# Filler products on TensorE around eight RMS norms of a three-block trunk

## The chip, the core and the metric

The kernel runs on one core of a Trainium2 chip. The time is that of one execution on the device, in microseconds (us); lower is better. TensorE is called PE here, VectorE DVE, ScalarE ACT, GpSimd POOL and SyncE SP. PEclk, the granted clock, is the share of full speed that the throttle granted to PE: 1.00 is 2.4 GHz and 0.50 is 1.2 GHz.

## What is computed

Two transformer layers over 256 context and 256 latent tokens of width 1024, then a third block of another kind. Each stage begins with an RMS norm and a modulation:

```python
def rmsnorm(x, w):
    x32 = x.astype(jnp.float32)
    r = lax.rsqrt(jnp.mean(x32 * x32, axis=-1, keepdims=True) + EPS)
    return (x32 * r).astype(x.dtype) * w

def trunk_layer(xl, xc, ...):
    xl = xl + 0.5 * g1l * swiglu(modulate(rmsnorm(xl, norm_w[0]), sh1l, sc1l), w_ffn1_in, w_ffn1_out)
    ...
    mix_l, mix_c = token_mixer(modulate(rmsnorm(xl, norm_w[1]), ...), ...)   # attention and a short convolution
    xl = xl + g2l * mix_l
    xl = xl + 0.5 * g3l * swiglu(modulate(rmsnorm(xl, norm_w[2]), sh3l, sc3l), w_ffn2_in, w_ffn2_out)
```

After the two layers comes a final norm. The third block takes its result: norm, two scans (mLSTM and HGRN) behind one input projection, output projection, norm, a feed-forward part with a convolution, final norm. In all there are ten norms.

## The kernel before

Everything is feature-major: x is 8 chunks (kc, 0 to 7) of 128 features by 512 tokens, in SBUF all the time. The weights come from HBM as units of 1 MB into a ring of three buffers (raw). SP starts the DMA for a unit when PE has begun the one that used its buffer (semaphore unit_begun). ACT splits each half of a unit into a high part (w_hi, line 877) and DVE into a low part (w_lo, line 1256), and PE makes three products for each chunk, high by high, high by low and low by high (split_product, lines 412 and 420). A product of 512 columns starts every 0.23 us, one of 256 every 0.12 us.

Each engine runs its own instruction list in the order written, and semaphores join them. PE's list is written by hand in the order of the stages.

A norm goes so. While the product before it still runs, DVE adds each finished chunk into x (line 1362, semaphore x_updated), ACT squares it (line 894, square_ready), and POOL adds the squares of chunks 0 to 5 into square_sum (line 1829, square_added). At the end of the product PE calls norm_sum. It sums over features by products with a column of ones, one for each 128 tokens (line 463, one column each, into bank 4): first POOL's sum (k = 0), then the squares of chunk 6 (k = 1), then those of chunk 7 (k = 2). ACT takes the root (line 904), DVE the reciprocal (1288) and four diagonal blocks of it (1290), and PE multiplies ones by these blocks, which spreads the factor over all partitions (line 471, "the spread", bank 5). DVE then scales x chunk by chunk (1309), ACT and DVE modulate (915, 1314), ACT makes the high part of h (919) and DVE the low part (1320). PE meanwhile runs joint_product (line 441): two weight halves side by side, each new chunk of h used as soon as it is there, the second half two chunks behind the first, 48 products in all.

The ten norms in order are norm10, norm20, norm30, norm11, norm21, norm31, final1, norm_a, norm_b and final2. norm31, final1, norm_b and final2 work on the 256 latent tokens alone (two blocks of 128 instead of four). The joint stage of norm21 has 256 columns, and that of norm_a 512 for one half and 256 for the other. norm_a follows final1 with no product between them. Behind norm_b comes no joint_product but f32 products straight from h and raw (line 821).

An f32 product stands in the trace as two records, each with its own weight load. Lines 463, 471 and 821 therefore have twice as many records as the code has products.

The eight PSUM banks are assigned by hand. Banks 2, 3, 6, 7, 0, 1, 2, 3 hold the eight chunks of a product ahead of a norm (OUT_BANK), so bank 6 holds the third. UPDATED[name] is how many updates of x stand ahead of a norm, and each adds 8 to x_updated.

Of the kernel before, what the change touches and what calls it, by code (L numbers as in the profile page):

```python
# [31 lines left out]
P = 128  # L32
D = 1024
KC = D // P
# [89 lines left out]
def build_program(nc, stream, x_in, ctx2_in, params_in, consts_in, out, until=None):  # L124
    with ExitStack() as stack:
        def sb(name, shape):
            return stack.enter_context(nc.sbuf_tensor(name, shape, F32))
# [8 lines left out]
        consts = sb("consts", [P, N_CONSTS])  # L136
# [17 lines left out]
        bank = [stack.enter_context(nc.psum_tensor(f"bank{b}", [P, 512], F32)) for b in range(8)]  # L154
        sems = {}

        def sem(name):
            if name not in sems:
                sems[name] = stack.enter_context(nc.semaphore(name))
            return sems[name]  # L160
# [5 lines left out]
        def const(name, a=0, n=None, rows=P):  # L166
            first, width = CONSTS[name]
            return consts[0:rows, first + a:first + a + (width - a if n is None else n)]

        ident, ones = const("ident"), const("ones")  # L170
# [8 lines left out]
        x_updated = sem("x_updated")  # L179
# [6 lines left out]
                 for i in range(DEPTH) for n in range(3)]  # L186
        NORMS += [("final1", 3 * DEPTH, CTX), ("norm_a", 3 * DEPTH + 1, 0), ("norm_b", 3 * DEPTH + 2, CTX),
                  ("final2", 3 * DEPTH + 3, CTX)]
        NORM_AT = {name: n for n, (name, _, _) in enumerate(NORMS)}
        UPDATED = {name: updates for name, updates, _ in NORMS}  # L190
        START = {name: t0 for name, _, t0 in NORMS}
        OUT_BANK = (2, 3, 6, 7, 0, 1, 2, 3)
        PAIR_BANKS = ((0, 1), (2, 3), (6, 7))
        ROW_BANK, TURN_BANK = 4, 5
        HEAD_NORM_BANK = (0, 1, 4, 5)
        SUM_BANK, SPREAD_BANK = 4, 5
        norm_rms, norm_rinv = small[:, 64:68], small[:, 68:72]
        ADDED = KC - 2
        square_sum = rinv
# [2 lines left out]
        def earlier(name, counts):  # L202

            return sum(1 for n, (other, _, t0) in enumerate(NORMS) if n < NORM_AT[name] and counts(other, t0))
# [8 lines left out]
        def joint(name):  # L213

            return name[:5] in ("norm1", "norm2", "norm3") or name == "norm_a"

        def diags_before(name):

            return sum((T - t0) // P for _, _, t0 in NORMS[:NORM_AT[name]])
# [158 lines left out]
        def _(pe):  # L378
# [71 lines left out]
            def normed(t0):  # L450
                return (lambda kc: h_hi[:, kc, t0:]), (lambda kc: h_lo[:, kc, t0:])

            def norm_sum(name):


                n, t0 = NORM_AT[name], START[name]
                for k, part in enumerate((square_sum, squares[:, 2, :], squares[:, 3, :])):
                    if k == 0:
                        pe.wait_ge(sem("square_added"), (ADDED - 1) * (n + 1))
                    else:  # L460
                        pe.wait_ge(sem("square_ready"), KC * n + ADDED + k)
                    for tc in range((T - t0) // P):
                        last = nc.tensor.matmul(bank[SUM_BANK][:, tc:tc + 1], part[:, t0 + tc * P:t0 + (tc + 1) * P], ones[:, 0:1],  # L463
                                                start=k == tc == 0, stop=k == 2, skip_group_check=True)
                        if k == tc == 0 and joint(name):
                            last.then_inc(half_begun, 1)
                last.then_inc(sem("norm_summed"), 1)
                if name == "norm10":
                    pe.wait_ge(sem("side_done"), FIRST_SIDES)
                pe.wait_ge(sem("diag_ready"), diags_before(name) + (T - t0) // P)  # L470
                nc.tensor.matmul(bank[SPREAD_BANK][:, 0:T - t0], ones, norm_diag[:, 0:T - t0], start=True, stop=True)\  # L471
                    .then_inc(sem("rinv_spread"), 1)

            def swiglu(name, norm, norm_after):
                f, t0 = FFNS.index(name), START[norm]
# [36 lines left out]
            def down(name, update, hidden_before, sides, t0, norm_after):  # L512

                before = KC * BANKED.index(update)
                operand = (lambda kc: hidden_hi[:, kc, t0:]), (lambda kc: hidden_lo[:, kc, t0:])
                for j in range(4 * len(GROUPS)):
                    at = AT[f"down{name}", j]
                    g, pair_of_chunks = j % len(GROUPS), j // len(GROUPS)
                    if j < sides:
                        side_sum(at - 1)  # L520
                    full_wait(pe, at)
                    pe.wait_ge(sem("hidden_ready"), hidden_before + min(KC * (g + 1), FC) if j < len(GROUPS) else hidden_before + FC)
                    if j == 3 * len(GROUPS):
                        pe.wait_ge(x_updated, before_updates(update) + 2)
                    for sub in range(2):
                        c = 2 * pair_of_chunks + sub
                        last = split_product(bank[OUT_BANK[c]][:, 0:T - t0], At.half, operand, GROUPS[g], KC * g, sub == 0,
                                             g == 0, g == len(GROUPS) - 1)
                        if g == len(GROUPS) - 1:
                            last.then_inc(sem("acc_ready"), 1)  # L530
                        if sub == 0 and j < sides:
                            side_turn(At.side)
                            At.side += 1
                norm_sum(norm_after)

            def out_product(name, update, t0, norm_after, await_chunk=None):

                for j in range(4):
                    full_wait(pe, AT[name, j])
                    if j == 0 and await_chunk:  # L540
                        for last in joint_product([bank[OUT_BANK[sub]][:, 0:T - t0] for sub in range(2)], [normed(t0)] * 2, await_chunk):
                            last.then_inc(sem("acc_ready"), 1)
                        continue
                    if j == 3:
                        pe.wait_ge(x_updated, before_updates(update) + 2)
                    for sub in range(2):
                        split_product(bank[OUT_BANK[2 * j + sub]][:, 0:T - t0], At.half, normed(t0), KC, 0, sub == 0)\
                            .then_inc(sem("acc_ready"), 1)
                norm_sum(norm_after)
# [294 lines left out]
            side_turn(FIRST_SIDES - 1)  # L844
            At.side = FIRST_SIDES
            norm_sum("norm10")
            for i in range(DEPTH):
                swiglu(f"1{i}", f"norm1{i}", f"norm2{i}")
# [1179 lines left out]
```

## Time and profile before

| | us |
|---|---|
| median of 3 runs | 2535.13 |
| lowest and highest | 2529.25, 2537.61 |
| span of the profiled execution | 2530.4 |
| PE busy in it | 2386.8 (94%) |
| DVE, ACT, POOL busy | 1163.3, 930.1, 172.2 |
| mean granted clock of PE | 0.969 |

The profiled execution is known by its span, from its first to its last instruction. That is 4.7 us under the median of the runs. A matmul record includes the time through the pipeline, so records of one engine overlap; the distance between their starts tells what a product costs.

### The profile page before, as it was taken

What the parts mean: (1) busy time and instruction counts of PE and PEld (TensorE: products, weight loads), DVE (VectorE), ACT (ScalarE), POOL (GpSimd) and SP (SyncE); (2) the same over time, 40 slices, a digit from 0 to 9 for tenths busy, and PEclk for the clock granted to TensorE, in tenths of its full rate; (3) what the DMA queues carried; (4) which work ended last, traced back from release to release, by engine and by line L of the source; (5) the groups of instructions that cost most, each with busy time, mean ns of one, the idle gap of its engine ahead of it and who ended that gap; (6) DMA issues with size and microseconds to landing.
All of it is one profiled execution on the core that took longest, in us unless ns stands there. A gap on an engine that the chain in (4) does not pass through costs nothing.

```text
span 2530.4 us, 34867 instructions
## 1 busy us (share of the span) xinstructions
PE 2386.8 (94%) x13140; PEld 1927.3 (76%) x13140; DVE 1163.3 (46%) x2058; ACT 930.1 (37%) x1446; POOL 172.2 (7%) x115
## 2 busy tenths in 40 slices
PE   6999999999999999999999999999997997789998
PEld 3777777784777777777777787779996876558888
DVE  2233222436643333224333224675545666656884
ACT  3333322323443333224333223356644364332333
POOL 1000000005010000010000000310001003101001
PEclk9999999999999999999999998999998998889999
DMA  6444445220134444443444433314553221004444
GB/s 241 166 166 166 166 167 191 88 88 34 35 116 166 166 166 166 169 185 129 166 166 166 166 117 112 121 67 150 182 196 104 100 100 67 1 26 141 150 148 167
DMA packets 47643, 340.50 MB, mean 135 GB/s; under 512 B 5184, under 2 KB 6208, under 8 KB 6592
## 3 DMA queue, kind: packets, MB, share of 16 engines
q1 hardware_dynamic: 47280, 338.19, 36.2%
q8 instruction: 64, 1.05, 0.2%
q0 software_dynamic: 272, 1.05, 0.1%
q14 instruction: 27, 0.22, 0.0%
HBM read 338.16 MB, written 1.05 MB: 134 GB/s over the span
## 4 chain that ended last, share of the span: by engine, by line
PE 89%; DVE 6%; ACT 2%; issue 1%; POOL 1%; DMA 0%; SPq 0%; DVEq 0%; ACTq 0%; POOLq 0%
PE bank L412 44%; PE bank L420 21%; PE bank L821 6%; PE bank L389 4%; PE bank L441 3%; PE bank L401 1%; PE bank L663 1%; PE bank L463 1%; PE bank L642 1%; DVE h L1601 1%; PE bank L622 1%; PE bank L651 1%; PE bank L619 1%; ACT w_hi L877 1%; PE bank L471 1%
## 5 line engine op out<-in xcount | busy, mean ns | idle before, releaser
L1256 DVE TENSOR_TENSOR w_lo<-raw,w_hi 128x1024 fp32r<-128x1024 f32 (+1 forms) x389 | 469.1, 1206 | 895.0 <-ACT w_hi L877 894.4
L877 ACT ACTIVATE w_hi<-raw 128x1024 fp32r<-128x1024 f32 (+1 forms) x389 | 403.3, 1037 | 853.9 <-DMA raw<-stream 436.8
L412 PE MATMUL bank<-h_hi,w_hi 128*128 128x512 f32 (+1 forms) x2024 | 709.7, 363 | 3.1 <-ACT w_hi L877 1.7
L412 PE MATMUL bank<-h_lo,w_hi 128*128 128x512 f32 (+1 forms) x2024 | 695.1, 356 | 0.0
L412 PEld LDWEIGHTS bank<-h_hi,w_hi 128*128 128x128 f32 x2024 | 383.6, 190 | 81.6 <-issue 28.3
L420 PE MATMUL bank<-h_hi,w_lo 128*128 128x512 f32 (+1 forms) x2024 | 429.8, 355 | 5.2 <-DVE w_lo L1256 5.2
L412 PEld LDWEIGHTS bank<-h_lo,w_hi 128*128 128x128 f32 x2024 | 383.9, 190 | 50.5 <-issue 0.5
L420 PEld LDWEIGHTS bank<-h_hi,w_lo 128*128 128x128 f32 x2024 | 341.3, 189 | 58.9 <-DVE w_lo L1256 6.0
L412 PE MATMUL bank<-hidden_hi,w_hi 128*128 128x512 f32 (+1 forms) x880 | 298.6, 354 | 2.5 <-ACT w_hi L877 2.5
L412 PE MATMUL bank<-hidden_lo,w_hi 128*128 128x512 f32 (+1 forms) x880 | 293.7, 348 | 0.0
L412 PEld LDWEIGHTS bank<-hidden_hi,w_hi 128*128 128x128 f32 x880 | 167.4, 190 | 32.8 <-issue 13.2
L420 PE MATMUL bank<-hidden_hi,w_lo 128*128 128x512 f32 (+1 forms) x880 | 182.0, 347 | 2.0 <-DVE w_lo L1256 2.0
L412 PEld LDWEIGHTS bank<-hidden_lo,w_hi 128*128 128x128 f32 x880 | 167.6, 190 | 19.5
L420 PEld LDWEIGHTS bank<-hidden_hi,w_lo 128*128 128x128 f32 x880 | 145.4, 190 | 22.8 <-DVE w_lo L1256 2.2
L821 PE MATMUL bank<-h,raw 128*128 128x256 f32 x704 | 153.9, 382 | 1.3 <-DVE h L1314 1.3
L821 PEld LDWEIGHTS bank<-h,raw 128*128 128x128 f32 x704 | 134.9, 192 | 20.6 <-issue 2.0
L1741 DVE SCALAR_TENSOR_TENSOR arena<-arena,params 128x189 f32<-128x189 f32 (+2 forms) x352 | 122.9, 427 | 20.2 <-ACT arena L1177 20.2
L1829 POOL TENSOR_TENSOR rinv<-squares 128x512 f32<-128x512 f32 (+1 forms) x10 | 15.1, 1514 | 1663.3 <-ACT squares L894 1663.3
L389 PE MATMUL bank<-raw,cond 128*32 128x256 f32 x1536 | 109.7, 406 | 18.2 <-DMA raw<-stream 14.5
L885 ACT ACTIVATE side_row<-bank 128x256 f32<-128x256 f32 x96 | 36.9, 385 | 242.3 <-PE bank L389 224.5
L1264 DVE TENSOR_TENSOR mod_ada<-bank,params 128x4 f32 (+1 forms) x72 | 11.7, 163 | 186.6 <-PE bank L401 186.6
L389 PEld LDWEIGHTS bank<-raw,cond 128*32 128x32 f32 x1536 | 41.6, 113 | 69.3 <-issue 34.6
(220 smaller groups left out, 2227.5 us busy)
## 6 DMA issues: line engine op xcount, KB each, us to landing
raw<-stream SPq DMA_DIRECT2D x318, 1024.0 KB, 4.8
x<-x_in SPq DMA_DIRECT2D x1, 2048.0 KB, 10.2
consts<-consts_in SPq DMA_DIRECT2D x1, 1121.5 KB, 5.8
x<-ctx_in POOLq DMA_DIRECT2D x1, 1024.0 KB, 6.1
out<-x SPq DMA_DIRECT2D x2, 512.0 KB, 3.0
params<-params_in SPq DMA_DIRECT2D x1, 413.5 KB, 3.2
```

The lines of the kernel that those rows point to most:

```text
L389: last = nc.tensor.matmul(bank[ROW_BANK][g:g + 32, 0:UNIT], cond[:, which, kc, :], raw[at % RING][:, kc, :], start=kc < 4, stop=kc >= 4)
L401: last = nc.tensor.matmul(bank[TURN_BANK][:, 2 * q:2 * q + 2], side_row[:, q * P:(q + 1) * P], const("sum_rows"), start=True, stop=True)
L412: last = nc.tensor.matmul(acc, w_hi[:, buffer, kc, :], v(first_chunk + kc), start=start and kc == n == 0, stop=False)
L420: last = nc.tensor.matmul(acc, w_lo[:, buffer, kc, :], hi(first_chunk + kc), start=False, stop=stop and kc == chunks - 1)
L441: last[sub] = nc.tensor.matmul(accs[sub], w[:, (At.half + sub) % 2, kc, :], v(kc), start=kc == n == 0, stop=kc == KC - 1 and n == 2)
L463: last = nc.tensor.matmul(bank[SUM_BANK][:, tc:tc + 1], part[:, t0 + tc * P:t0 + (tc + 1) * P], ones[:, 0:1], start=k == tc == 0, stop=k = ...
L471: nc.tensor.matmul(bank[SPREAD_BANK][:, 0:T - t0], ones, norm_diag[:, 0:T - t0], start=True, stop=True)\
L821: last = nc.tensor.matmul(bank[PAIR_BANKS[j][gv]][:, 0:LAT], raw[at % RING][:, kc, gv * P:(gv + 1) * P], h[:, kc, CTX:], start=kc == 0, st ...
L877: nc.scalar.activation(w_hi[:, buffer, 0:chunks, :], raw[at % RING][:, 0:chunks, sub * P:(sub + 1) * P], ACT.Copy)\
L885: nc.scalar.activation(side_row[:, :], bank[ROW_BANK][:, 0:UNIT], ACT.Copy).then_inc(sem("side_row"), 1)
L1256: nc.vector.tensor_tensor(w_lo[:, buffer, 0:chunks, :], raw[at % RING][:, 0:chunks, sub * P:(sub + 1) * P], w_hi[:, buffer, 0:chunks, :].b ...
L1741: nc.vector.scalar_tensor_tensor(acc[:, ro, co], source[:, ri, ci], w, acc[:, ro, co], ALU.mult, ALU.add)\
```

## The change

norm_sum gets filler products at three places, for the eight norms ahead of which x was updated, except final2: norm20, norm30, norm11, norm21, norm31, final1, norm_a and norm_b. A filler multiplies the identity by 256 columns of constants, in f32, into bank 6, which nobody reads before it is written anew. Two stand between the sum with k = 0 and the wait for the sum with k = 1, four between the sums and the wait for the spread's diagonals, and eight behind the spread. A new wait at the top of norm_sum holds PE until four of the eight chunks have been added into x, so that bank 6 is free.

```diff
+        KEEP_BANK = 6
+        KEEP = (2, 4, 8)
...
+            def keep_running(count):
+
+                for _ in range(count):
+                    nc.tensor.matmul(bank[KEEP_BANK][:, 0:2 * P], ident, consts[:, 0:2 * P], start=True, stop=True)
+
             def norm_sum(name):
 
 
                 n, t0 = NORM_AT[name], START[name]
+                busy = UPDATED[name] > 0 and name != "final2"
+                if busy:
+                    pe.wait_ge(x_updated, KC * UPDATED[name] - 4)
                 for k, part in enumerate((square_sum, squares[:, 2, :], squares[:, 3, :])):
                     if k == 0:
                         pe.wait_ge(sem("square_added"), (ADDED - 1) * (n + 1))
                     else:
+                        if k == 1 and busy:
+                            keep_running(KEEP[0])
                         pe.wait_ge(sem("square_ready"), KC * n + ADDED + k)
...
                 last.then_inc(sem("norm_summed"), 1)
+                if busy:
+                    keep_running(KEEP[1])
                 if name == "norm10":
                     pe.wait_ge(sem("side_done"), FIRST_SIDES)
                 pe.wait_ge(sem("diag_ready"), diags_before(name) + (T - t0) // P)
                 nc.tensor.matmul(bank[SPREAD_BANK][:, 0:T - t0], ones, norm_diag[:, 0:T - t0], start=True, stop=True)\
                     .then_inc(sem("rinv_spread"), 1)
+                if busy:
+                    keep_running(KEEP[2])
```

## Rows read from the trace of the kernel before

**Rows 1.** The page: the span, busy times by engine, the chain by engine.
```profile
span 2530.4 us, 34867 instructions
...
PE 2386.8 (94%) x13140; PEld 1927.3 (76%) x13140; DVE 1163.3 (46%) x2058; ACT 930.1 (37%) x1446; POOL 172.2 (7%) x115
...
PE 89%; DVE 6%; ACT 2%; issue 1%; POOL 1%; DMA 0%; SPq 0%; DVEq 0%; ACTq 0%; POOLq 0%
```

**Rows 2.** Waits of PE, whole span: total us, times, longest us.
```profile
PE bank L471 <- DVE rms L1290: 13.8, 10, 1.6
...
PE bank L463 <- POOL rinv L1829: 9.8, 1, 9.8
```

**Rows 3.** Timeline, norm11: start us, us, engine, line, operation [idle before <-releaser].
```profile
1143.05 0.95 PE L463 MATMUL bank<-consts,rinv 128*128 128x1 f32 x8
1143.86 2.04 PE L463 MATMUL bank<-consts,squares 128*128 128x1 f32 x16
1147.44 2.08 PE L471 MATMUL bank<-rms,consts 128*128 128x512 f32 x2 [1.54 <-DVE rms L1290]
...
1152.14 0.76 PE L441 MATMUL bank<-h_hi,w_hi 128*128 128x512 f32 x1 [2.62 <-ACT h_hi L919]
...
1159.65 0.69 DVE L1320 TENSOR_TENSOR h_lo<-squares,h_hi 128x512 fp32r<-128x512 f32 x1
...
1165.28 0.39 PE L441 MATMUL bank<-h_lo,w_hi 128*128 128x512 f32 x1
```

**Rows 4.** Stretches: us, busy of PE, PEld, DVE, ACT, POOL, then PEclk, DMA, GB/s.
```profile
471.00:471.50 0.50, 0.27 (x2) 0.18 (x1) 0.00 (x0) 0.19 (x2) 0.00 (x0) 0.50 0.00 0
...
717.50:719.50 2.00, 0.62 (x6) 0.53 (x5) 1.01 (x6) 1.21 (x2) 0.00 (x0) 1.00 0.00 0
...
724.30:729.50 5.20, 5.20 (x12) 3.50 (x13) 5.20 (x11) 4.05 (x8) 0.00 (x0) 0.50 0.57 202
...
1716.90:1726.40 9.50, 7.78 (x29) 6.54 (x30) 9.23 (x25) 3.40 (x9) 0.00 (x0) 0.50 0.35 113
...
1927.30:1932.50 5.20, 5.20 (x24) 5.18 (x24) 0.00 (x0) 0.00 (x0) 0.00 (x0) 0.50 0.00 0
...
2294.20:2300.00 5.80, 4.54 (x10) 3.22 (x11) 4.57 (x14) 0.00 (x0) 0.00 (x0) 0.50 0.12 24
```

**Rows 5.** Groups by line and shape, PE: busy us, mean ns | idle before.
```profile
L821 PE MATMUL bank<-h,raw 128*128 128x256 f32 x704 | 153.9, 382 | 1.3 <-DVE h L1314 1.3
```

**Rows 6.** Timeline, norm31: sums, spread, last joint product.
```profile
1714.53 1.19 PE L463 MATMUL bank<-consts,squares 128*128 128x1 f32 x8
1716.86 1.22 PE L471 MATMUL bank<-rms,consts 128*128 128x256 f32 x2 [1.14 <-DVE rms L1290]
...
1728.98 0.28 PE L441 MATMUL bank<-h_lo,w_hi 128*128 128x256 f32 x1
```

**Rows 7.** Timeline, final1 and norm_a.
```profile
1915.11 0.61 PE L463 MATMUL bank<-consts,squares 128*128 128x1 f32 x4 [0.24 <-ACT squares L894]
1916.79 0.70 PE L471 MATMUL bank<-rms,consts 128*128 128x256 f32 x2 [1.07 <-DVE rms L1290]
1927.29 1.86 PE L463 MATMUL bank<-consts,rinv 128*128 128x1 f32 x8 [9.81 <-POOL rinv L1829]
...
1934.14 2.07 PE L471 MATMUL bank<-rms,consts 128*128 128x512 f32 x2 [1.58 <-DVE rms L1290]
```

**Rows 8.** Timeline, norm_b: spread, first products of line 821, last chunks of h.
```profile
2294.17 1.22 PE L471 MATMUL bank<-rms,consts 128*128 128x256 f32 x2 [1.14 <-DVE rms L1290]
2296.66 3.69 PE L821 MATMUL bank<-h,raw 128*128 128x256 f32 x8 [1.26 <-DVE h L1314]
...
2300.03 0.74 DVE L1314 TENSOR_SCALAR h<-h,scales,mod_mod 128x256 f32<-128x256 f32 x2
```

**Rows 9.** Timeline, norm30: spread and last joint product.
```profile
719.66 2.00 PE L471 MATMUL bank<-rms,consts 128*128 128x512 f32 x2 [1.54 <-DVE rms L1290]
...
737.90 0.39 PE L441 MATMUL bank<-h_lo,w_hi 128*128 128x512 f32 x1
```

## Prediction

> **What bounds the kernel now.** I read the page first: PE is busy for 94% of the span and carries 89% of the chain that ended last [rows 1], so what PE does is the time, and at a norm the question is only what PE waits for. The waits of PE come next. Before the spread product (line 471) it waited for DVE's diagonals, 13.8 us over ten norms, and once 9.8 us for POOL's sum of squares [rows 2]. Then I went through each norm by its timeline. Norm11 stands for four alike (norm20, norm30, norm11, norm21: 512 columns). Its sums (line 463) run from 1143.05 to 1145.9, the spread comes 1.54 us later and takes 2.08 us, the first product of the joint stage comes 2.62 us after that, and the last of its 48 products starts at 1165.28 [rows 3]. Last I cut the time by granted clock. It was 1.00 up to the end of the sums, or nearly, and 0.50 (1.2 GHz instead of 2.4) in the spread, in the wait behind it and in the first microseconds of the joint products [rows 4]. At norm_a the sums ran back to back for 5.2 us and the clock stayed at 0.50, so those one-column products did not bring it back, while the dense products of lines 441 and 821 did [rows 4].
>
> **What is added and its price.** Eight norms get 2, 4 and 8 fillers (norm20, norm30, norm11, norm21, norm31, final1, norm_a, norm_b): 112 products; norm10 and final2 get none. A filler is an f32 product of 128 by 128 with 256 columns. The same form stands in line 821: 704 records, two for each product, in 153.9 us [rows 5], so 153.9 / 352 = 0.44 us each. At half clock eight records took 3.69 us [rows 8], 0.85 us for a product after the first. So the three places cost PE 0.87, 1.75 and 3.50 us at full clock, and up to 1.7, 3.4 and 6.8 us at half clock. The new wait on x_updated asks for half of the chunks, while the wait right behind it needs the squares of six of them: it ends earlier, I count it as nothing, and if it did cost its place is ahead of the sums in each norm. Bank 6 has been read by then, so nobody waits for the fillers but PE's own queue.
>
> **First place, 2 fillers between the first sum and the second.** In the full-width norms there is no wait to fill: the 24 records of line 463 follow each other without idle time, as in norm11 [rows 3]. All 0.87 us goes on the path, with bounds of 0.55 (norm20, where the clock fell inside the old sums already and part of that comes back) and 0.87. Four norms: 3.2 us. In the half-width ones the third sum waited 0.24 us for ACT [rows 7], so 0.87 minus about 0.3 = 0.57. At norm_a PE comes from 9.81 us of idling at half clock and the squares are long there [rows 7]: 1.7 us.
>
> **Second place, 4 fillers between sums and spread.** Here there is a real wait, 1.54 us by the records plus about 0.17 of pipeline end [rows 3]: at full clock 1.75 fills it with 0.05 over. In the half-width norms the wait is 1.07 to 1.14 plus 0.17 [rows 6, 7], so 0.45 us too much. At half clock the four take 3.4 us and delay the spread by 1.7.
>
> **What it should give back.** Spread at full clock: a half-width one took 0.70 us at final1 at clock 1.00 and 1.22 us at norm31 [rows 6, 7]; 0.52 us less, and twice that, 1.04, for 512 columns. Joint stage of the four: in norm11 the sixth chunk's low part is ready at 1160.34 [rows 3], 22 products stand behind it at 0.228 us each, 5.0 us, which gives 1165.4; the stage ended at 1165.51. So norm11 has 0.1 us to gain, and I take the same for norm20. In norm30, at half clock for over 5 us of it [rows 4], the last product starts 16.24 us after the spread's end, in norm11 15.76 us [rows 3, 9]: 0.5 us. Norm21, half-width in its joint stage, I put beside norm30: 0.5. That is 1.2 us in all. Here the expected gift is mostly absent: DVE's pace of 1.52 us a chunk hides the slow products.
>
> **Third place, 8 fillers after the spread.** PE was idle there for 2.62 us [rows 3]; 3.50 us make the first joint product about 0.7 us late. In the full-width norms this costs nothing, as the first two chunks need only three products each (0.7 us of 1.52) and PE is back in step with DVE before the third. Norm31 has half-width products: PE would be free 3.33 + 48 x 0.12 = 9.1 us after the spread, DVE's pace gives 9.7, measured 11.0 at half clock up to past 1726.4 [rows 4, 6], so 1.3 us comes back, less 0.5 us (0.57 + 0.45 - 0.52) by which the spread is later now: minus 0.8. At norm_b line 821 started 1.26 us after the spread and PE sets its pace [rows 8]. Before, half clock until about 2300 put the eighth product's end at 2301.9. After, the spread ends 0.5 us later here too, PE is free at 2299.1, and eight products end at 2302.6: plus 0.7. Final1 was at full clock already: 0.57 + 0.45 = plus 1.0, its eight hidden under 9.81 us of idling. Norm_a: 1.7 + 1.7, less 0 to 1.0 at the spread [rows 7]: plus 3.0, with 2.4 to 3.4 as bounds.
>
> **Does the clock hold?** No row shows this schedule. In the four full-width norms 0.9 us of sums, 0.87 of fillers and 1.8 of sums stand in a row. Before, the clock fell in some norms while the sums still ran and in others only after the wait (0.50 at 471.0, 1.00 at 719.5) [rows 4], so its fall is not tied to a place in the code. If it falls in the sums or at the second place, the four fillers and the spread lose 1.1 to 1.7 us, and up to 3.2 if it stays down longer. The bounds are nothing and 3.2 for each norm; I take a fall in every second norm at 1.7, since the nearest rows show both outcomes: 2 x 1.7 = 3.5 us. The half-width norms have sums of half the length, and I take the clock to hold in norm31 and norm_b.
>
> The page "TensorE: Matmul & The Clock Gate" of the Trainium skill, Part 1, says that the throttled state is the default and that activity lifts it; on that reading any filler helps, and by it the clock would hold everywhere. The trace agrees that dense products lift it and that idling drops it, but not that all products do: norm_a's sums did not. The same page (Part 2, step 1) says that matmuls stay in program order and only weight loads are pulled ahead. That speaks against this change: a filler whose successor is ready delays it by its whole length, and the sum by it is the one above.
>
> **Sum.** Full-width norms: 3.2 (first) + 0.2 (second) - 4.2 (spread) - 1.2 (joint) + 3.5 (falls) = +1.5. Norm31 -0.8, final1 +1.0, norm_b +0.7, norm_a +3.0. In all +5.4 us. The profiled span is 2530.4 us, 4.7 under the median of the three runs, 2535.13; 2530.4 + 5.4 = 2535.8 for a span, 2540.5 us for the median.
>
> **Rivals.** (a) Forecast, mixed: +5.4, from +3 to +9. Chance 0.55. (b) The clock holds everywhere but at the start of norm_a: no falls, norm_a +2.4: -2.0 - 0.8 + 1.0 + 0.7 + 2.4 = +1.3, 2536.4 us. For it: dense products stand in every gap. Against: three stretches of sums remain. Chance 0.17. (c) The clock falls in nearly every norm, because the sums count for as little as idling does: four times 2.0 more than (b), norm31 +0.9, norm_b +1.7, norm_a +3.4: +13, 2548 us, slower. It decides from the point where the clock is down when the second place begins, since those four then take 3.4 us in a wait of 1.7. Chance 0.19. (d) Faster: a filler costs less than a product of line 821, as all fillers share one weight tile. At half the price (0.22 us) the second place is hidden, the first costs 0.4 and norm_b's third ends near its h: about -6 us, 2529 us. Against: each product there has its own two weight loads, and the loads were shorter than the products. Chance 0.06. (e) It does not do what it says: constants do not count as activity, PE stays at half clock through all three places, 10 us or more go to them in each norm and 3 to 4 us of that are exposed even under DVE, so 25 to 40 us slower. Chance 0.03.
>
> **How the numbers follow.** A measurement of this kernel tells about 0.3%, 7.6 us, from no change. Slower by more than that: (c), (e) and the upper tail of (a), 0.29. Faster by more: the far side of (d), 0.04. Within: 0.67. The range takes (a) with both bounds, (b), (c) and some of (d), and the spread of single times, 8 us in the three runs: 2533 to 2549.
>
> **What would show it.** First place right: line 463 is split by two fillers and ends 0.5 to 0.9 us later after the last big product. Second: the spread starts within 0.1 us of the diagonals in norms with clock 1.00, 1.7 us late in those at 0.50. Give-back: a 512-column spread near 1.04 us instead of 2.08. Third: the joint stage of norm30 ends no later after its spread than before. The forecast is wrong if the fillers show up at 0.2 us each, if the clock reads 1.00 from the sums to the joint products in all eight norms, or if the stages between norms change.

## The result, and the profile after

| | before | after |
|---|---|---|
| median of 20 runs, us | 2535.13 | 2541.53 |
| lowest and highest | 2529.25, 2537.61 | 2534.39, 2547.23 |
| ratio, with 95% interval | | 1.0031 (1.0024 to 1.0038) |
| span of the profiled execution | 2530.4 | 2538.0 |
| mean granted clock | 0.969 | 0.977 |

The change makes the kernel 6.4 us slower by the medians. The ratio is not the quotient of the two medians: 1.0031 stands for 7.9 us and its interval for 6.1 to 9.6. The three runs of the table ahead of the prediction are the first three of the 20. The granted clock went up and the waits that the fillers were put into went down, and the time went up all the same. In after an execution's time is its span plus 1.8 us (2538.0 and 2539.8), and with the same sum the profiled execution of before took 2532.2 us. So it was 2.9 us faster than the median of its kernel, and that of after 1.7 us. In the kernels with fillers (those with the edit of after) lines 441, 463 and 471 of before have the numbers 443, 475 and 485, lines 724, 733 and 821 have 740, 749 and 837, and a filler is line 458; in fitted, further down, the numbers behind the fillers are two lower.

The page of after, against [rows 1]. PE has 224 records more, the 112 fillers, and is busy 34 us longer.

```profile
span 2538.0 us, 35323 instructions
...
PE 2420.5 (95%) x13364; PEld 1961.1 (77%) x13364; DVE 1169.2 (46%) x2058; ACT 930.8 (37%) x1446; POOL 166.7 (7%) x115
```

The waits of PE in after (what is waited for, total us, times, longest), against [rows 2]. The wait for the diagonals fell from 13.8 us in ten norms to 2.7 in the two norms without fillers, and that for POOL at norm_a from 9.8 to 6.5 (fillers fill the rest). As waits, all of this looks like a gain.

```profile
PE bank L475 <- POOL rinv L1845: 6.5, 1, 6.5
...
PE bank L485 <- DVE rms L1306: 2.7, 2, 1.6
```

The groups of PE in after by line and shape (busy us, mean ns, idle before).

```profile
L837 PE MATMUL bank<-h,raw 128*128 128x256 f32 x704 | 152.1, 379 | 0.0
...
L458 PE MATMUL bank<-consts 128*128 128x256 f32 x224 | 56.3, 399 | 0.0
```

A filler record is as long as one of the like product of line 837: sharing one weight tile makes it no cheaper (399 and 379 ns). Now norm11 in time (start, us, engine and line, operation, idle before), to be held against [rows 3]:

```profile
1142.45 0.95 PE L475 MATMUL bank<-consts,rinv 128*128 128x1 f32 x8
1143.26 1.11 PE L458 MATMUL bank<-consts 128*128 128x256 f32 x4
1144.21 1.84 PE L475 MATMUL bank<-consts,squares 128*128 128x1 f32 x16
1145.91 1.97 PE L458 MATMUL bank<-consts 128*128 128x256 f32 x8
1147.72 1.02 PE L485 MATMUL bank<-rms,consts 128*128 128x512 f32 x2
1148.58 3.62 PE L458 MATMUL bank<-consts 128*128 128x256 f32 x16
1151.85 0.58 PE L443 MATMUL bank<-h_hi,w_hi 128*128 128x512 f32 x1
...
1164.51 0.39 PE L443 MATMUL bank<-h_lo,w_hi 128*128 128x512 f32 x1
```

And the granted clock (the number behind the busy times) in the same norm and at norm_a:

```profile
1143.00:1146.00 3.00, 3.00 (x25) 2.90 (x25) 1.74 (x4) 0.63 (x1) 0.00 (x0) 1.00 0.00 0
1146.00:1151.00 5.00, 5.00 (x23) 3.97 (x23) 4.41 (x11) 2.71 (x5) 0.00 (x0) 1.00 0.00 0
1151.00:1153.00 2.00, 2.00 (x11) 1.66 (x9) 2.00 (x5) 1.66 (x4) 0.00 (x0) 1.00 0.00 0
1927.00:1932.00 5.00, 5.00 (x21) 4.64 (x21) 0.00 (x0) 0.00 (x0) 0.00 (x0) 0.50 0.01 3
1932.00:1938.00 6.00, 6.00 (x18) 4.77 (x19) 2.19 (x6) 1.21 (x2) 0.00 (x0) 0.50 0.00 0
1938.00:1944.00 6.00, 5.82 (x24) 4.34 (x23) 5.03 (x10) 3.85 (x7) 0.00 (x0) 0.94 0.01 5
```

The reader is to see three things. First, the clock held at 1.00 from the sums to the first joint products of norm11, where it had been 0.50 in the spread and in the first joint products. Second, the norm takes from its first sum to the last joint product 1164.51 - 1142.45 = 22.06 us, where it took 1165.28 - 1143.05 = 22.23 [rows 3]. Full clock through a norm is worth 0.17 us: the fillers ahead of the spread push its start back by 0.88, the spread itself gives 1.06 back, and the joint stage takes 15.8 us after the spread as before. DVE sets its pace there: its low parts of h came every 1.52 us in both traces. Third, norm_a stays at 0.50 under six fillers, and pays for them:

```profile
1926.74 1.83 PE L475 MATMUL bank<-consts,rinv 128*128 128x1 f32 x8 [6.45 <-POOL rinv L1845]
1928.44 2.05 PE L458 MATMUL bank<-consts 128*128 128x256 f32 x4
1930.28 3.41 PE L475 MATMUL bank<-consts,squares 128*128 128x1 f32 x16
1933.56 3.76 PE L458 MATMUL bank<-consts 128*128 128x256 f32 x8
1937.11 1.82 PE L485 MATMUL bank<-rms,consts 128*128 128x512 f32 x2
```

From the first sum to the spread's start it was 6.85 us [rows 7], and is 10.37 here.

Each norm measured in this way (first sum to start of the last joint product, us; for norm_a the last of the 48 is taken, for final1 the end is norm_a's first sum, for norm_b final2's) in two traces of the changed kernel and three in which the code of the first five norms is the old one (of the third, called late below, the last three columns are left out, since it has fillers there):

| | norm20 | norm30 | norm11 | norm21 | norm31 | final1 | norm_a | norm_b |
|---|---|---|---|---|---|---|---|---|
| before | 22.48 | 22.63 | 22.23 | 20.26 | 15.05 | 13.37 | 23.18 | 228.96 |
| copy of before | 21.60 | 22.64 | 22.22 | 20.25 | 13.87 | 13.37 | 23.19 | 229.19 |
| late | 22.22 | 21.67 | 21.83 | 20.21 | 14.94 | | | |
| after | 22.06 | 22.06 | 22.06 | 20.06 | 14.34 | 14.43 | 26.46 | 229.56 |
| after, second trace | 22.06 | 22.06 | 23.76 | 21.74 | 14.34 | 14.43 | 26.33 | 229.56 |

The five norms of before differ by up to 1.2 us among traces of the same code. After against before, this is -0.42, -0.57, -0.17, -0.20, -0.71, +1.06, +3.28 and +0.60, together +2.9 us of the 7.6 us between the two spans. Another 4.2 us lie in none of the norms, but in the stage of the second scan between norm_a and norm_b: 340.77 us in before, 344.99 in after. The two traces differ there in two ways. One is the products of line 733, which took 7.17 us in before:

```profile
2182.33 2.05 PE L724 MATMUL bank<-arena,h 128*128 128x128 f32 x16 [2.58 <-DVE h L1608]
2185.80 7.17 PE L733 MATMUL bank<-arena 128*128 128x256 f32 x32 [1.42 <-DVE arena L1633]
```

and 9.06 in after, from where its first 3.1 us ran at half clock:

```profile
2186.70 2.73 PE L740 MATMUL bank<-arena,h 128*128 128x128 f32 x16 [2.58 <-DVE h L1624]
2190.86 9.06 PE L749 MATMUL bank<-arena 128*128 128x256 f32 x32 [1.42 <-DVE arena L1649]
```

The granted clock of that stretch:

```profile
2190.90:2194.00 3.10, 3.10 (x7) 2.48 (x8) 0.00 (x0) 0.00 (x0) 0.00 (x0) 0.50 0.00 0
```

That is 1.9 us of the 4.2. The other way stands ahead of it, where DVE and POOL both prepare h for the products of line 724. In before one POOL instruction took 8.51 us, and PE waited for it:

```profile
2128.97 8.51 POOL L1871 TENSOR_TENSOR h<-h,arena 128x1024 f32<-128x1024 f32 x1 [4.44 <-ACT h L1108]
...
2137.62 6.44 PE L724 MATMUL bank<-h 128*128 128x128 f32 x32 [5.83 <-POOL h L1871]
```

In after the same instruction took 2.46 us, and PE waited for DVE, where one instruction of line 1601 (1617 in after) took 2.84 us instead of 0.71:

```profile
2131.72 2.46 POOL L1887 TENSOR_TENSOR h<-h,arena 128x1024 f32<-128x1024 f32 x1 [4.44 <-ACT h L1124]
...
2136.60 3.68 PE L740 MATMUL bank<-h 128*128 128x128 f32 x16 [1.97 <-DVE h L1633]
```

Counted from norm_a's last joint product, line 724 began after 187.15 us in before and after 183.40 in after, and from its first to its last product it took 46.8 and 52.8 us. Together that is the other 2.3 us. The code of this stage is the same in both kernels. Whether the 4.2 us belong to the change is what the copy of before was run for.

### The profile page after: what moved, and what is told of

Same layout as the page of the kernel before. It is cut to its first block, busy times and chain, and to the rows that moved or that the text cites. A ratio compares the mean times of both kernels' runs of the same rounds, so it can differ in the third digit from the quotient of the medians.

```text
span 2538.0 us, 35323 instructions
## 1 busy us (share of the span) xinstructions
PE 2420.5 (95%) x13364; PEld 1961.1 (77%) x13364; DVE 1169.2 (46%) x2058; ACT 930.8 (37%) x1446; POOL 166.7 (7%) x115
## 3 DMA queue, kind: packets, MB, share of 16 engines
q0 software_dynamic: 272, 1.05, 0.1%
HBM read 338.16 MB, written 1.05 MB: 134 GB/s over the span
## 4 chain that ended last, share of the span: by engine, by line
PE 89%; DVE 7%; ACT 2%; issue 1%; DMA 0%; POOL 0%; SPq 0%; DVEq 0%; ACTq 0%; POOLq 0%
PE bank L414 44%; PE bank L422 21%; PE bank L837 6%; PE bank L391 4%; PE bank L443 2%; PE bank L403 1%; DVE h L1617 1%; PE bank L458 1%; PE bank L679 1%; PE bank L475 1%; PE bank L658 1%; PE bank L638 1%; DVE squares L1325 1%; PE bank L667 1%; PE bank L635 1%
```

## The experiments

All kernels of one group ran on the same chip beside the kernel before, whose medians there were 2534.47 (25 runs), 2535.18 (26) and 2534.70 (28).

### First group: which norms

**copy** is the kernel before, unchanged.

> The kernel before, unchanged, as a second sample of its trace. Theory A (the HGRN stage's length changes from execution to execution): its trace may show from 63 to 68 us between the end of the input projections and the end of the HGRN products, while norms agree with the first trace within 0.5 us; ratio 1.000. If the stage is as before to 0.3 us here and 4 us longer in late, Theory B or B' stands.

Measured: 2536.04 us, ratio 1.0006 (0.9997 to 1.0016), span of its trace 2532.5. The trace:

```profile
2181.04 2.54 PE L724 MATMUL bank<-arena,h 128*128 128x128 f32 x16 [2.58 <-DVE h L1608]
2185.00 9.26 PE L733 MATMUL bank<-arena 128*128 128x256 f32 x32 [1.42 <-DVE arena L1633]
```

The unchanged code shows the long form of line 733 too, and 344.91 us for the stage. Over the thirteen traces of this study that stage took 340.8 to 347.1 us with the same instructions, twelve of them 344.1 or more. So the 4.2 us aren't shown to be an effect of fillers: the profiled execution of before was the one with the shortest stage.

The form with POOL and DVE is another matter, since it goes with the kernel and not with the execution. POOL's instruction took 8.5 us in the five traces of before, copy, late, first_only and second_only, and 2.5 us in the other eight, all of kernels with fillers behind the spread at the early norms. In those eight line 724 begins 3.7 us earlier than in copy and takes longer, 52.8 us in after where copy had 48.8, and in five of them the stage comes out at 344.9 to 345.0 us, as in copy. The three stages over 346 us are all among the eight. So a kernel with fillers up to norm31 has two other engines meet differently some 400 us later. Why is open, and what it costs on the average no run here shows.

Against the copy, after is 5.5 us longer by span, of which norm_a and final1 carry 4.3.

**late** has the fillers at final1, norm_a and norm_b alone.

```diff
-                busy = UPDATED[name] > 0 and name != "final2"
+                busy = name in ("final1", "norm_a", "norm_b")
```

> Fillers only at final1, norm_a and norm_b, 2, 4 and 8 as in the changed kernel. Theory A: 1.1 + 3.3 + 0.6 = 5 us slower, ratio 1.0020, the HGRN stage as long as before on the average of runs. Theory B' (the fillers at norm_a are what makes the HGRN stage longer, by clock or by the order in which DVE and POOL meet there): 9 us slower, ratio 1.0036. If the five early norms were what cost the time, ratio 1.000.

Measured: 2537.61 us, 1.0014 (1.0003 to 1.0026), 3.1 us more than before. In its trace final1 is at +1.05, norm_a +2.25 (here the clock rose during the four fillers, 3.48 us instead of 3.76, and the spread took 1.02), norm_b +0.60: 3.9 us. The three norms are slower by about what they show (5 us was expected, and the interval reaches from 0.8 to 6.6).

**five** has them at norm20, norm30, norm11, norm21 and norm31 alone.

```diff
-                busy = UPDATED[name] > 0 and name != "final2"
+                busy = name in ("norm20", "norm30", "norm11", "norm21", "norm31")
```

> Fillers 2, 4 and 8 only at norm20, norm30, norm11, norm21 and norm31; none at final1, norm_a and norm_b. In the changed kernel's trace those five ended their joint stages 0.2 to 0.7 us earlier after their first sum than before, 2.1 us in all. Theory A (the loss lies at final1, norm_a and norm_b, about 5 us, and what the HGRN stage lost, 4.2 us, is chance of the execution): 2 us faster than before, ratio 0.9992. Theory B (any filler ahead shifts the HGRN stage into its longer form): 2 us slower, ratio 1.0008, with the HGRN stage 4 us longer. Theory C (the clock holds only by chance in the one profiled execution and falls in others): ratio 1.001 and over, with the clock at 0.50 at a norm in the trace.

Measured: 2542.01 us in 5 runs, 1.0035 (1.0021 to 1.0049). Its trace has four of the five norms as in after and one fall of the clock (norm21, 21.73). Two microseconds faster was expected and 7.5 slower was measured, so the early norms aren't free. The traced execution was the fastest of the five, so it doesn't show where the others lost their time. The kernel was therefore run again as **five_again**:

> The kernel five once more. Its timed executions were 2538 to 2543.8 us, over the 2536 of the one whose trace is kept. Theory C (falls of the clock come in more of the five norms in most executions): the trace has two or more norms of the five with four fillers of over 3 us, and the five together are 2 us or more longer than in the first trace. Theory E (the longer executions lose it in the HGRN stage, by the clock): the five norms agree with the first trace within 1 us and the stretch from norm_a to norm_b is longer than 345 us. Ratio 1.002 to 1.004 by either.

Measured: 2538.79 us in 11 runs, 1.0018 (1.0006 to 1.0029), 4.1 us more. Its trace has no fall in any of the five norms (22.06, 22.07, 22.10, 20.05, 14.34), and the stage between norm_a and norm_b took 346.95 us, the one behind norm_b 231.18 instead of 229. That is what theory E expected: no falls in the norms, a stage of over 345 us. The five norms cost something, 4.1 and 7.5 us in the two comparisons; the traces show some 1.7 us for each fall and 0.5 for a fall at final1, where this kernel has no fillers (its spread took 1.22 us in five, 0.70 in before). Against the copy the trace of five_again is 5.4 us longer, and 4.0 of these lie between norm_a's joint stage and final2, where this kernel has no fillers. Whether fillers ahead put them there isn't shown.

**five_no_first** is five without the two fillers of the first place.

```diff
-        KEEP = (2, 4, 8)
+        KEEP = (0, 4, 8)
```

> As five, but without the two fillers between the first and the second sum. Theory A (in a place with no wait a filler costs its whole length, 0.87 us in four norms and 0.57 us in norm31, and the clock holds or falls late enough without it): 3 to 4 us faster than five, 5 to 6 us faster than before, ratio 0.9978. Rival D (the first place is what keeps the clock up: without it the clock falls in the sums, the four fillers take 3.4 us and the spread 2 us): no faster than five, ratio 0.9992 to 1.001, spreads of 2 us in the trace.

Measured: 2539.00 us, 1.0019 (1.0008 to 1.0030): 3.0 us less than five beside it, but the same ratio as five_again, and the intervals of the two overlap. Faster than before by 5 to 6 us was expected, and it was 4.5 slower. Norm20 and norm11 took 21.29 us in its trace, 0.77 less than with the first place, which is close to the 0.87 that two fillers cost; norm30 and norm21 had a fall of the clock (22.97 and 20.99). So the first place is paid nearly in full where the clock holds, and it doesn't stop the falls for sure, as norm21 of five shows.

### Second group: which place

**first_only**, **second_only** and **third_only** (the last with the third group) keep one place at all eight norms.

```diff
-        KEEP = (2, 4, 8)
+        KEEP = (2, 0, 0)   # first_only
+        KEEP = (0, 4, 0)   # second_only
+        KEEP = (0, 0, 8)   # third_only
```

> Only the two fillers between the first and the second sum, at all eight norms. By the prediction's step each costs its whole length there: 3.2 us at the four full-width norms, 0.5 at each of norm31, final1 and norm_b, 1.7 at norm_a, and nothing comes back, since the spread and the wait behind it stay at half clock: 6.4 us slower, ratio 1.0025, and the spread 2.0 us long in the trace. Rival: two fillers are enough to carry the clock over to the spread, 1 us back in each of four norms: 2.4 us slower, ratio 1.0009, spreads near 1.0 us.

Measured: 2546.5 us in 6 runs, 1.0046 (1.0034 to 1.0058), 11.3 us more, more than the whole change. Its trace, the fastest of the six, shows norm_a at +1.7, final1 and norm31 at +0.6 and +0.4 and the wait for the diagonals back at 13.8 us:

```profile
1144.37 1.11 PE L458 MATMUL bank<-consts 128*128 128x256 f32 x4
1145.32 1.84 PE L475 MATMUL bank<-consts,squares 128*128 128x1 f32 x16
1148.71 1.12 PE L485 MATMUL bank<-rms,consts 128*128 128x512 f32 x2 [1.55 <-DVE rms L1306]
1152.46 0.76 PE L443 MATMUL bank<-h_hi,w_hi 128*128 128x512 f32 x1 [2.62 <-ACT h_hi L935]
```

The norms of this trace add up to +3.6 us against before. The spread was expected to stay at 2.0 us. It took 1.12 us in norm11, as above, and 1.49 in norm20, but 2.08 and 2.07 in norm30 and norm21: the rival's mechanism, that two fillers carry the clock to the spread, is seen in some norms. The first place is the worst of the three, which was expected; that it costs 11 us in the timed runs wasn't, and the trace doesn't explain it.

> Only the four fillers between sums and spread, at all eight norms. Theory A (they cost nothing at full clock and win the spread back): where the clock holds a full-width norm is 1.0 us shorter, where it falls 0.5 us longer, as in the trace of five_no_first; norm31, final1 and norm_b lose 0.5 us each and win 0.5 in two of them, norm_a loses 1.7: between 2 us faster and 4 us slower, ratio 0.9992 to 1.0015, middle 1.0005. Theory C (the clock is mostly down there in executions other than the one profiled): 1.7 us lost in each norm, ratio 1.004.

Measured: 2537.02 us, 1.0003 (0.9990 to 1.0017): nothing that can be told from zero, with single runs from 2527.6 to 2543.8, the widest spread of all. The trace has both cases. Norm30 and norm11 took 21.30 us; in norm20 the clock fell before the fillers and they ran 1.7 us over:

```profile
469.37 2.03 PE L475 MATMUL bank<-consts,squares 128*128 128x1 f32 x16
471.26 3.56 PE L458 MATMUL bank<-consts 128*128 128x256 f32 x8
474.62 1.16 PE L485 MATMUL bank<-rms,consts 128*128 128x512 f32 x2
```

> Only the eight fillers behind the spread, at all eight norms. They start at half clock, since nothing ahead of the spread holds it, and last up to 6.8 us in a wait of 2.8. By the prediction's steps the full-width norms lose 0 to 1 us each (DVE's pace hides most), norm31 0 to 2, norm_b 2 to 5 (line 837 has no such cover), norm_a 0 to 1, final1 nothing: 5 us slower, ratio 1.002, from 1.001 to 1.004. Rival (the dense fillers bring the clock up before the joint products, and so nothing is lost): ratio 0.9995 to 1.0005.

Measured: 2536.20 us, 1.0008 (0.9999 to 1.0018), 1.5 us more, where 5 was expected. In norm11 the clock was low as the eight fillers began, and they brought it up (eight in 4.6 us, the joint products behind them at full clock). The first joint product starts 5.92 us after the spread does, where it was 4.70 in before [rows 3], so the fillers run 1.2 us past the first h. That is hidden by DVE's pace: norm11 took 21.70 us, 0.1 less than the quickest of the old form.

```profile
1146.72 1.53 PE L485 MATMUL bank<-rms,consts 128*128 128x512 f32 x2 [1.54 <-DVE rms L1306]
1148.05 4.94 PE L458 MATMUL bank<-consts 128*128 128x256 f32 x16
1152.64 0.58 PE L443 MATMUL bank<-h_hi,w_hi 128*128 128x512 f32 x1
```

At norm_b there is no such cover. The eight fillers began at half clock and took 6.0 us, so that line 837 began 7.01 us after the spread's start, where it was 2.49 in before [rows 8]. The norm took 231.69 us, 2.7 more, in the expected range of 2 to 5:

```profile
2294.87 1.22 PE L485 MATMUL bank<-rms,consts 128*128 128x256 f32 x2 [1.14 <-DVE rms L1306]
2295.88 6.16 PE L458 MATMUL bank<-consts 128*128 128x256 f32 x16
2301.88 4.48 PE L837 MATMUL bank<-h,raw 128*128 128x256 f32 x20
```

**after_again** is the changed kernel once more, for a second trace.

> The changed kernel once more, for a second trace of it. Theory A: the early norms read as in the first trace, 22.06 us from first sum to last joint product, final1 to norm_a 14.4, norm_a 26.5, and ratio 1.002 to 1.0035. Theory C (the clock's falls are a matter of phase and differ by execution): one or more of the four full-width norms has four fillers that take over 3 us, and is 1 to 2 us longer than in the first trace.

Measured: 2541.77 us, 1.0028 (1.0018 to 1.0037), span 2540.7. In norm11 and norm21 the clock fell, in the same code that held it at 1.00 there in the first trace. Norm11:

```profile
1143.88 1.84 PE L475 MATMUL bank<-consts,squares 128*128 128x1 f32 x16
1145.58 3.30 PE L458 MATMUL bank<-consts 128*128 128x256 f32 x8
1148.67 1.43 PE L485 MATMUL bank<-rms,consts 128*128 128x512 f32 x2
1149.94 3.62 PE L458 MATMUL bank<-consts 128*128 128x256 f32 x16
```

And the clock of the stretch in which it was down:

```profile
1145.50:1149.80 4.30, 4.30 (x12) 3.11 (x13) 2.19 (x6) 1.21 (x2) 0.00 (x0) 0.60 0.00 0
```

Four fillers took 3.09 us instead of 1.81, the spread came that much later and took 1.43 instead of 1.02, and the whole norm took 23.76 instead of 22.06: 1.70 us for a fall. That is the term of the prediction, seen in 2 of 8 full-width norms of the two traces, in 3 of 16 when five and five_again are added (they have the same counts there).

### A version whose fillers fit even at half clock

**fitted** has no first place, no fillers at final1, and counts that end before the diagonals at full clock and little after them at half.

```diff
-        KEEP = (2, 4, 8)
+        KEEP = {"norm20": (2, 3), "norm30": (2, 3), "norm11": (2, 3), "norm21": (2, 3), "norm31": (1, 2), "norm_a": (2, 3), "norm_b": (1, 1)}
...
-                busy = UPDATED[name] > 0 and name != "final2"
+                busy = name in KEEP
...
-                        if k == 1 and busy:
-                            keep_running(KEEP[0])
...
-                    keep_running(KEEP[1])
+                    keep_running(KEEP[name][0])
...
-                    keep_running(KEEP[2])
+                    keep_running(KEEP[name][1])
```

> None at the first place, none at final1; 2 and 3 fillers at the second and third place of the full-width norms and norm_a, 1 and 2 at norm31, 1 and 1 at norm_b. Each count fits its wait at half clock too (two take 1.7 us of 1.7, three 2.6 of 2.8). Theory A (the changed kernel loses by fillers that outlast their wait): no norm longer than before, 0 to 1 us back where the clock holds: 1 to 4 us faster, ratio 0.9985 to 1.000. Theory C' (without the first place the clock falls in the sums in every norm): ratio 1.000, spreads of 2 us. If it is slower by over 0.1%, the loss is not in what fillers outlast.

Measured: 2533.49 us, 0.9993 (0.9984 to 1.0001). It was run again as **fitted_again**, in the third group:

> The kernel fitted once more. If its small gain is real, the ratio is again 0.998 to 1.000 and both intervals together leave 1.000 out or nearly; if it was chance of the executions, 1.000 to 1.001.

Measured: 2534.14 us, 0.9999 (0.9990 to 1.0007). Norm11 in the trace of fitted:

```profile
1145.37 1.11 PE L458 MATMUL bank<-consts 128*128 128x256 f32 x4
1147.05 1.12 PE L483 MATMUL bank<-rms,consts 128*128 128x512 f32 x2 [0.57 <-DVE rms L1304]
1148.01 1.46 PE L458 MATMUL bank<-consts 128*128 128x256 f32 x6
1150.80 0.47 PE L443 MATMUL bank<-h_hi,w_hi 128*128 128x512 f32 x1 [1.33 <-ACT h_hi L933]
```

Here a wait of 0.57 us is left ahead of the spread, and 1.33 us ahead of the joint products: the fillers are wholly inside waits. The norm took 21.28 us, 0.95 less than in before, in the other trace 21.95. No cost is left that the timed runs show, and 0.6 to 1.7 us of the whole kernel came back, which isn't told apart from nothing; 1 to 4 us were expected. In other norms the clock did fall (norm30's spread came 0.2 us late and took 1.74), and little was lost by it. The clearest gain is at norm_b, where PE sets the pace: from the first sum to the last product of line 821 it was 158.94 us in before and 157.97 in both traces of this version. This is the size of what these counts win here. Seven of the eight norms keep the new wait on x_updated, and the stretch from norm30's last joint product to norm11's first sum is 405.15 us in all thirteen traces, so that wait isn't what costs.

## Why the prediction was right, point by point

**The total.** 2540.5 was forecast and 2541.5 measured, in the range. That the two lie so close is luck in part: the gains and the falls of the clock were both put too high, and the two errors cancel, as told below.

**The price of a filler.** 0.44 and 0.85 us were put in. In norm11 four fillers move the next product by 1.81 us, eight by 3.27: 0.41 to 0.45 us each at full clock. At norm_a four took 1937.11 - 1933.56 = 3.55, 0.89 each at half. Rival (d) falls.

**First place.** 0.87 us in each full-width norm was forecast; the sums of after end 3.60 us after the first, of before 2.85, so 0.75, and leaving the place out gave 0.77 back. The place is dearest, as the sum said, but the timed runs of first_only (11.3 us) say more than the sum did (6.4 us expected for it alone).

**Second place and spread.** At full clock the spread of norm11 starts 5.27 us after the first sum, before 4.39. Of these 0.88 the first place has 0.75, which leaves 0.13 for the second (0.05 was forecast). It takes 1.02 us, forecast 1.04. The half-width ones take 0.59 (0.70 was forecast).

**Joint stage.** Forecast 0.1 us for norm11 and norm20, 0.5 for norm30 and norm21. Against before norm20, norm30 and norm11 gave 0.42, 0.57 and 0.17, where the terms for the place, the spread and the joint stage add up to 0.54, 0.62 and 0.22; norm21 gave 0.20 where 0.62 stood, so its 0.5 was wrong: it lay like norm11, not like norm30. The main reading holds for the full-width norms: DVE's pace of 1.52 us a chunk hides products at half clock.

**The half-width norms and norm_a.** Norm31 -0.71 (forecast -0.8), final1 +1.06 (+1.0), norm_b +0.60 (+0.7), norm_a +3.28 and +3.15 (+3.0). These four terms carried the sum, and late confirms three of them together at +3.1 us timed.

**Falls of the clock.** This term was mis-sized. A fall costs 1.7 us as put in, but it came in a quarter of the full-width norms of the changed kernel and not in half of them: 1.7 us for an execution instead of 3.5. In the profiled trace there was none, and norm by norm it is rival (b): clock at 1.00 in all norms but norm_a, +2.9 us, where (b) had +1.3 with norm_a at 2.4. Against this, the gains in the five early norms were oversized too, since they were reckoned from one trace of before. The mean of three traces with the old code in the first five norms is 22.10, 22.31, 22.09, 20.24 and 14.62, and beside these the five norms of after without a fall give only 0.8 us, where before alone says 2.1. With -0.8 + 1.7 + 1.1 (final1) + 3.1 (norm_a) + 0.5 (norm_b) the sum is +5.6 us, against 6.4 and 6.6 between the medians of the two comparisons (7.9 and 7.1 by the ratios). Falls came in some executions and not in others, so the case (a), mixed, fits best; how often they come rests on four traces.

**The base.** The prediction took 4.7 us, from the profiled span to the median, for something that lies around every span. Only 1.8 lie around it; 2.9 was the luck of that execution, with its short stage of 340.8 us. As the sum was added to the median in the end, no harm came of it, but the 2535.8 for a span was too low: 2538.0 and 2540.7 were seen.

**What the text said would change.** "If the stages between norms change" was given as a sign against the forecast. They do change. Between norm_a and norm_b it is up to 6.3 us over all traces, 4.1 of them between the two traces of the kernel without fillers. Behind the last product of line 821 the stage takes 70.0 or 71.5 us, and both are seen in the traces of five and of fitted. A single pair of traces can't tell this from the change. Two things, though, go with the kernel in every trace: the meeting of POOL and DVE told of at copy, and the stretch from norm21's end to norm31, which took 138.7 or 138.8 us in before, copy, after, five and five_no_first and 137.4 in the other kernels. The prediction had no term for either.

**The clock rule.** The page "TensorE: Matmul & The Clock Gate" of the Trainium skill, Part 1, says that throttling is the default state and activity releases it. The traces agree for fillers in a row (third_only: 1.53 us for the spread ahead of them, full clock behind). It doesn't follow that a low clock costs time: the rule speaks of the clock, and the full-width norms are bound by DVE while it is low. The same page of the Trainium skill, Part 2, step 1, says that matmuls stay in program order. The trace agrees: at norm11 four fillers moved the next product by 1.81 us, their whole length. This is the rule that priced the change.

**What stays open.** The single places add up to 11.3 + 1.8 + 1.5 = 14.6 us where the whole change costs 6.4, and five and first_only are slower when timed than their traces account for, by some 4 to 8 us. More falls of the clock in the untraced executions don't explain this. The mean granted clock is on record for each execution, and one fall as in norm11 of after_again (4.30 us at 0.60) lowers it by 0.0007. Of the executions of five, those of 2536.04 and 2542.01 us both had 0.973, and those of 2537.99, 2543.48 and 2543.76 us all had 0.971, where 6 us more by falls of 1.7 us each would ask for at least 0.002 less. The six of first_only had 0.962 on the average, as the kernel before had beside them. The stages outside the norms that come in short and long forms could hold the difference, if a small shift changes how often each form comes. That is argued and not shown: it would take traces of the slower executions.

## What to carry to other kernels

Filling a wait of TensorE to keep its clock is worth at most what PE-bound work at half clock stands behind the wait; where another engine sets the pace there, it is near nothing (0.17 us in norm11), and only the costs are left. A filler where the next product is ready costs its full length, so count the fillers by the shortest wait at half clock, and put none at a place without a wait (the first place moved the spread by 0.75 us in a full-width norm). Before a difference of a few us between two traces is put down to an edit, trace the unchanged kernel twice: here one stage alone moved by 4 us. And look at the other engines too: here the busy time of DVE rose by 5.9 us and that of POOL fell by 5.5, in a stage that the edit doesn't touch.

## What the runs showed of the hardware

One-column sums mixed with fillers lifted the clock late: at norm_a, after an idle wait of 6.45 us, PE was busy without a gap from 1926.74 to 1937.11 and the clock stayed at 0.50 for these 10 us in after, while in late it rose during the last four fillers. The same instruction list gave a clock of 1.00 in norm11 in one execution and 0.60 over 4.30 us of it in another. One POOL instruction of the scan took 8.5 us in five traces and 2.5 in eight, with DVE's beside it at 0.7 and 2.8 us. And f32 products of 128 by 128 by 256 with one and the same weight tile cost what they cost with changing tiles, 0.41 to 0.45 us, each with its own two weight loads.
